# Modulation rows in four places, state space heads in another order, and inverse blocks interleaved over the array's quadrants

## What is computed

```python
# block 1
proj = rms_norm(h) @ w_in
y_ssd  = ssd_mixer(...)      # 8 heads of 64, 4 chunks of 128 tokens
y_rwkv = rwkv7_mixer(...)    # 8 heads of 64, a recurrence over tokens:
#   S = S * w_t + (S a_t) b_t^T + v_t k_t^T ;  y_t = S r_t
h = h + rms_norm(concat(y_ssd, y_rwkv) @ w_out)
f = (silu(gate) * val) @ ffn_w_down      # after a depthwise conv of rms_norm(h) @ w_up
h = h + rms_norm(f)
# block 2
mod = silu(c) @ w_mod + b_mod            # 6 * 1024 numbers for shifts, scales and gates
h = h + gate1 * hybrid_mixer(rms_norm(h) * (1 + scale1) + shift1)
h = h + gate2 * experts(rms_norm(h) * (1 + scale2) + shift2)
```

## Time and profile before

| | |
|---|---|
| runs of the kernel | 2032.84, 2038.69, 2039.38 us; median 2038.69 |
| profiled execution, its own time | 2028.1 us |
| its span | 2026.3 us |
| busy share of the span | TensorE 89%, weight loads 69%, VectorE 60%, GpSimd 34%, ScalarE 24% |
| mean granted clock of TensorE | 0.923 |

### The profile page before, as it was taken

How to read it: one execution, slowest core, us unless ns; L and a number is a source line. 1 busy time by engine, 2 the same in 40 slices (tenths; PEclk the granted TensorE clock), 3 DMA queues, 4 the chain that set the end, 5 groups by cost and what they waited for, 6 DMA issues and landing times.

```text
span 2026.3 us, 28621 instructions
## 1 busy us (share of the span) xinstructions
PE 1812.8 (89%) x11514; PEld 1393.4 (69%) x11514; DVE 1224.7 (60%) x1599; ACT 491.4 (24%) x734; POOL 679.9 (34%) x383
## 2 busy tenths in 40 slices
PE   6999666998887999999979999989898998699998
PEld 4888345777665777777738788877676775466665
DVE  6959236564438888888760276728734442566664
ACT  2121322442112111101131111312133103354443
POOL 2664000000152666666526556004433562100000
PEclk8999567999798999999989999659999999799999
DMA  5231222222023222322212222001311225488884
GB/s 196 83 104 63 83 84 66 105 86 97 14 80 115 87 101 83 103 83 89 77 42 84 83 83 83 1 1 63 120 42 63 83 84 207 178 348 343 333 334 176
DMA packets 34066, 230.47 MB, mean 114 GB/s; under 512 B 4132, under 2 KB 4388, under 8 KB 8232
## 3 DMA queue, kind: packets, MB, share of 16 engines
q1 hardware_dynamic: 30240, 214.48, 29.2%
q10 hardware_dynamic: 2136, 10.24, 1.3%
q0 software_dynamic: 1584, 4.21, 0.6%
HBM read 220.98 MB, written 9.50 MB: 114 GB/s over the span
## 4 chain that ended last, share of the span: by engine, by line
PE 73%; DVE 15%; DMA 5%; ACT 3%; issue 3%; POOL 0%; SPq 0%; DVEq 0%; ACTq 0%; POOLq 0%
PE psum L383 72%; DVE arena L1465 4%; DVE arena L1471 4%; DMA arena<-units 2%; DVE arena L1468 2%; DMA weight_ring<-units 2%; PE psum L387 1%; ACT arena L1119 1%; DVE tiny L1479 1%; ACT L1119 1%; DVE expert_lo L1465 1%; ACT expert_hi L1119 0%; ACT tiny L1119 0%; DMA arena<-x 0%; POOL slots L2321 0%
## 5 line engine op out<-in xcount | busy, mean ns | idle before, releaser
L1119 ACT ACTIVATE arena<-psum 128x512 f32<-128x512 f32 (+4 forms) x295 | 149.2, 520 | 901.0 <-PE psum L383 789.8
L383 PE MATMUL psum<-arena 64*64 64x64 f32 (+4 forms) x2828 | 270.4, 290 | 59.9 <-DVE arena L1465 45.7
L383 PEld LDWEIGHTS psum<-arena 64*64 64x64 f32 (+3 forms) x2828 | 194.9, 171 | 117.6 <-issue 67.1
L383 PE MATMUL psum<-normed_hi,w_in_hi 128*128 128x512 f32 x512 | 204.3, 399 | 14.3 <-DVE in_lo L1465 8.3
L1465 DVE TENSOR_TENSOR arena<-arena,psum 128x512 f32<-128x512 f32 (+2 forms) x200 | 112.2, 588 | 151.8 <-PE psum L383 103.5
L383 PE MATMUL psum<-normed_hi,w_in_lo 128*128 128x512 f32 x512 | 203.3, 397 | 0.0
L383 PE MATMUL psum<-in_lo,w_in_hi 128*128 128x512 f32 x512 | 201.8, 394 | 0.0
L1471 DVE SCALAR_TENSOR_TENSOR arena<-arena,fixed_data 128x512 f32<-128x512 f32 x134 | 188.9, 1410 | 13.5 <-DVE arena L1468 0.2
L2279 POOL TENSOR_TENSOR w_ff_lo<-weight_ring,w_ff_hi 128x1024 fp32r<-128x1024 f32 x66 | 166.6, 2524 | 5.5
L2279 POOL TENSOR_TENSOR w_in_lo<-weight_ring,w_in_hi 128x1024 fp32r<-128x1024 f32 x64 | 163.1, 2548 | 5.4
L383 PE MATMUL psum<-arena,fixed_data 128*128 128x512 f32 (+10 forms) x424 | 130.6, 474 | 36.4 <-DVE arena L1465 18.0
(11 more groups left out here) (226 smaller groups left out, 3527.2 us busy)
## 6 DMA issues: line engine op xcount, KB each, us to landing
weight_ring<-units SPq DMA_DIRECT2D x124, 1024.0 KB, 4.8
arena<-units SPq DMA_DIRECT2D x55, 1024.0 KB, 7.5
normed<-units SPq DMA_DIRECT2D x20, 1024.0 KB, 8.1
slots<-arena ACTq DMA_DIRECT2D x7, 516.0 KB, 5.1
arena<-slots SPq DMA_DIRECT2D x7, 516.0 KB, 5.8
fixed_data<-fixed ACTq DMA_DIRECT2D x1, 2944.0 KB, 12.0
arena<-x SPq DMA_DIRECT2D x4, 512.0 KB, 5.9
arena<-bias_rows ACTq DMA_DIRECT2D x2, 896.0 KB, 5.7
```

The source lines that it names most:

```text
L383: return nc.tensor.matmul(o, l, r, start=start, stop=stop)
L1119: return nc.scalar.activation(o, i, func, **kw)
```

## The change

- **Modulation**: of the 24 units, 10 stand in the state space stage (two ahead of the loop, then one behind each head's 7 matmuls), 10 in the pairs (levels 2 and 4; in the fourth pair levels 1 to 4), 2 behind the sum after the output projection and 2 behind the sum after the feed-forward (`last_modulation`, with its own row buffers and its own columns). SyncE's order of loads follows: the last four units are taken out of their place in memory when their turn comes. GpSimd begins to split the feed-forward's weights, and later those of the second projection, when the second of these rows is in PSUM, where it waited for the last tile of the output projection or of the feed-forward.
- **State space heads**: `cs_row(h + 2)` stands ahead of head h's matmuls, `s_HB` has four buffers, the other right-hand side is written in place, ScalarE and VectorE run `decay_row` and `log_decays` two heads ahead.
- **Pairs**: a transposed copy of the first gram is computed as one more gram (`abT_crossed`, 16 matmuls of 64 x 64), with its output halves crossed; U is computed from half to other half, Z U from a half to the same half and X U from a half to the other, and Z U and X U of one head alternate, two matmuls each. `gt` and `hh` alternate in the same way, behind a wait for `aww`. VectorE makes the same number of operations.
- The four MEMSETs stand ahead of the squares of the output projection.

```diff
+            def last_modulation(g):
+
+                for j in range(2):
+                    rows_of_unit(N_MOD1 + 2 * g + j, W_MOD2_UNITS[g] + j, 5 + j)
+                o = open_("mod_columns", g, 7)
+                for j in range(2):
+                    emptied(pe, "mod_rows", N_MOD1 + 2 * g + j)
+                    for c in range(2):
+                        last = mm(o[:, 2 * j + c:2 * j + c + 1], mod_rows2[j][:, c * P:(c + 1) * P], sel4[:, :])
+                close(last, "mod_columns", g)
 
+            modulation(0)
+            modulation(1)
             for h in range(8):
                 m, e = h // 2, h % 2
-                modulation(h)
+                if h + 2 < 8:
+                    cs_row(h + 2)
                 if e == 0:
...
-                if h + 2 < 8:
-                    cs_row(h + 2)
+                modulation(2 + h)
                 if 1 <= h < 6:
                     prepare(0, h, 4)
             for g in range(2):
...
+            def block(o, q, e, t, l, r):
+
+                return mm(c8(o)[rows_of(q[1]), t, :], c8(half(l, e))[rows_of(q[0]), t, :], c8(half(r, e))[rows_of(q[0]), t, :])
...
+                        o = open_((f"U{lv}", m), e, 3 * e)
+                        for t in range(NT):
+                            for i in range(2):
+                                last = block(o, (1 - i, i), e, t, r_LV, r_X)
+                        close(last, (f"U{lv}", m), e)
...
                         emptied(pe, (f"U{lv}", m), e)
-                        blocks(f"ZU{lv}", m, e, 3 * e + 1, r_U, r_Z)
+                        oz = open_((f"ZU{lv}", m), e, 3 * e + 1)
                         if lv < 5:
-                            blocks(f"XU{lv}", m, e, 3 * e + 2, r_Z, r_U)
+                            ox = open_((f"XU{lv}", m), e, 3 * e + 2)
+                        for t in range(NT):
+                            for i in range(2):
+                                z = block(oz, (i, i), e, t, r_U, r_Z)
+                            if lv < 5:
+                                for i in range(2):
+                                    x = block(ox, (i, 1 - i), e, t, r_Z, r_U)
+                        close(z, (f"ZU{lv}", m), e)
+                        if lv < 5:
+                            close(x, (f"XU{lv}", m), e)
                     if m < 3:
                         prepare(m + 1, lv, 6)
...
                 emptied(pe, "awa", m)
-                o = open_("gt", m, 2)
+                emptied(pe, "aww", m)
+                og, oh_ = open_("gt", m, 2), open_("hh", m, 5)
...
             def decay_row(h):
                 filled(act, "cs_row", h)
                 f(xn[:, h, :], PSB[bank_of("cs_row", h)], ACT.Exp).then_inc(sem("row_decay_ready"), 1)
 
+            decay_row(0)
+            decay_row(1)
+            mod_row(0)
+            mod_row(1)
             for h in range(8):
-                decay_row(h)
                 emptied(act, "cs_row", h)
-                f(A(s_HB + (h % 2) * T), A(s_HB + (h % 2) * T), ACT.Exp).then_inc(sem("pair_decay_ready"), 1)
+                f(A(s_HB + (h % 4) * T), A(s_HB + (h % 4) * T), ACT.Exp).then_inc(sem("pair_decay_ready"), 1)
+                if h + 2 < 8:
+                    decay_row(h + 2)
                 if 2 <= h < 7:
                     prepare(0, h - 1)
-                mod_row(h)
+                mod_row(2 + h)
             for m in range(4):
                 f(proj(ZZ + m), proj(ZZ + m), ACT.Silu).then_inc(sem("z_ready"), 1)
             for g in range(2):
@@ -1239,8 +1279,8 @@
                         evac((f"U{lv}", m), e, half(r_U, e), PSB[bank_of((f"U{lv}", m), e)][:, 0:256])
                     if lv == 1:
                         evac("wv", m, r_WV)
-                    if lv < 5:
-                        mod_row(8 + 4 * m + lv - 1)
+                    if lv in (2, 4) or (m == 3 and lv in (1, 3)):
+                        mod_row(10 + 2 * m + (lv - 1 if m == 3 else lv // 2 - 1))
                     if m < 3:
                         prepare(m + 1, lv)
...
             for h in range(8):
-                if h + 1 < 8:
-                    log_decays(h + 1)
                 dve.wait_ge(sem("pair_decay_ready"), h + 1)
-                tt(A(s_CE + (h % 2) * T), proj(CM + h // 4), xn[:, h, :], ALU.mult)
-                tt(A(s_HB + (h % 2) * T), A(s_HB + (h % 2) * T), A(s_GT + (h // 4) * T), ALU.mult)\
+                tt(xn[:, h, :], proj(CM + h // 4), xn[:, h, :], ALU.mult)
+                tt(A(s_HB + (h % 4) * T), A(s_HB + (h % 4) * T), A(s_GT + (h // 4) * T), ALU.mult)\
                     .then_inc(sem("mt_ready"), 1)
+                if h + 2 < 8:
+                    log_decays(h + 2)
                 if h >= 2:
...
-                masked_gram("abT", m, r_AT, k_strict)
+                masked_gram("abT", m, r_Z, k_level[0])
+                masked_gram("abT_crossed", m, r_AT, k_strict)
                 for e in range(2):
                     emptied(dve, ("abT", m), e)
-                link(tt(c8(r_Z), c8(r_AT), rep8(k_level[0]), ALU.mult))
+                link(tt(c8(r_Z), c8(r_Z), rep8(k_ident), ALU.add))
                 masked_gram("ab", m, r_X, k_level0t)
-                link(tt(c8(r_Z), c8(r_Z), rep8(k_ident), ALU.add))
+                for e in range(2):
+                    emptied(dve, ("abT_crossed", m), e)
                 for e in range(2):
                     emptied(dve, ("ab", m), e)
...
 
+            V.memset(A(F_UB, 4 * PADW).rearrange("p (t c) -> p t c", t=4)[:, :, 0:3], 0.0).then_inc(sem("ffn_zeroed"), 1)
+            link(V.memset(A(F_ACC, 4096), 0.0))
+            link(V.memset(A(F_CMB, ROW), 0.0))
+            V.memset(A(F_CMB + D + 4, 1).bitcast(I32), T).then_inc(sem("empty_row_ready"), 1)
             for k in range(KT):
                 emptied(dve, "mix", k)
                 tt(sq(k), n_(k), n_(k), ALU.mult).then_inc(sem("sq_post_mix"), 1)
             rstd("sum_post_mix", 1.0 / D, 1e-6)
             add_normed(n_, "g_post_mix")
-            V.memset(A(F_UB, 4 * PADW).rearrange("p (t c) -> p t c", t=4)[:, :, 0:3], 0.0).then_inc(sem("ffn_zeroed"), 1)
-            link(V.memset(A(F_ACC, 4096), 0.0))
-            link(V.memset(A(F_CMB, ROW), 0.0))
-            V.memset(A(F_CMB + D + 4, 1).bitcast(I32), T).then_inc(sem("empty_row_ready"), 1)
+            def last_mod(g):
+
+                c = slice(40 + 4 * g, 44 + 4 * g)
+                filled(dve, "mod_columns", g)
+                tt(mod[:, c], PSB[7][:, 0:4], S("b_mod", 40 + 4 * g, 4), ALU.add).then_inc(freed("mod_columns", g), 1)
+
+            last_mod(0)
             rstd("sum_pre_ffn", 1.0 / D, 1e-6)
             scaled_parts(in_ff, lambda k: S("g_pre_ffn", k), "ffn_in_ready")
...
 
-            unit[0] += N_MOD
+            unit[0] += N_MOD1
 
             filled(pool, "ry_w", 3)
             split_units(w_out1, 4)
 
-            filled(pool, "mix", KT - 1)
+            unit[0] += 2
+            filled(pool, "mod_rows", N_MOD1 + 1)
             split_units(w_ff, 3 * NF)
-            filled(pool, "ffn_down", ("last", 0, KT - 1))
+            unit[0] += 2
+            filled(pool, "mod_rows", N_MOD1 + 3)
             split_units(w_in2, 18)
 
             pool.wait_ge(sem("gla_out_ready"), 4)
```

105 lines of the change are left out of this document (59 added, 46 removed).

## The result

The changed kernel takes 2010.65 us (median of four runs, 2002.60 to 2015.99) against 2035.76 (2032.33 to 2039.38) for the kernel before, run beside it: a ratio of 0.9873, 95% interval 0.9827 to 0.9919. The forecast was 2003, the range 1984 to 2020. The gain forecast was 35.6 us; the medians show 25, and the two profiled executions 22.2 (spans 2026.3 and 2004.1). So the sign and the range hold, and about a third of the gain is missing. The runs of the changed kernel spread over 13 us, those of the kernel before over 7. Repeated later, the changed kernel took 2011.77 beside 2029.92 for the kernel before: 18.2 us less, half of the forecast.

The account below looks back on a forecast made before the run. TensorE was taken to bound the kernel, holding 73% of the chain of waits. Heads -22, pairs -21, output projection +2 and feed-forward +5.4 sum to -35.6 us: 2003 against the median of 2038.69, range 1984 to 2020.

Parts of the forecast that it names:

- the place where VectorE should start (275.1): Behind the state space heads: VectorE starts at 275.1 instead of 297.1, minus 22 us (ends minus 5.5, minus 32).
- the collision: Behind both projections: GpSimd's weight splits slow VectorE's additions, 2.8 us a chunk, plus 5.5 and 5.4; bounds nothing and 5.6.
- First head at 213: State space stage: the first head's matmuls start some 1.2 us earlier than the 214.22 of before.
- The seven ways in 55 us: State space loop, first to last head's matmuls: 55 us instead of 79.6, between 47 all high clock and 70 all low.
- the circle at the high clock: State space heads at 2.4 GHz: matmuls, modulation, ScalarE's copy and exponential, VectorE's two products follow each other in 5.9 us.
- the rival of the low clock: State space heads stay TensorE's own work at 1.2 GHz and win only 5.5 us: 2019.5; chance 0.12.
- The end, 4.1 to 5.4 us: Behind head 7: VectorE waits 4.1 to 5.4 us for modulation, copy, table switch and first silu, instead of 0.1.
- The pairs, minus 21: Head pairs: minus 6.5 us for each of the first three, minus 1.3 for the fourth; bounds 13 and 25.
- its fall as a rival: Head pairs: more gaps bring TensorE down to 1.2 GHz, 27 us a pair, 2111 with all four; chance 0.02.
- Four quadrants, 1.16 us for 64 records: Pairs' levels: Z U and X U in four quadrants run at the grams' 1.16 us instead of 2.02, minus 0.8.
- The rival with the shared banks: Pairs: four quadrants with shared banks do not run side by side, 14 us less gain: 2017; chance 0.1.
- MEMSETs, minus 3.4: Behind the output projection: MEMSETs leave VectorE's path, so the next norm starts at 617.2 instead of 620.59, minus 3.4 us.

Follow-up runs that it names:

- the later splits: Changed kernel with GpSimd's first splits for the feed-forward and second projection waiting until VectorE has added the last modulation's columns; median 2007.91 us, ratio 0.9874.

## Why the prediction was right, and where its sizes were off

- **The range and the sign** hold, and the range by luck in part. The likeliest values were too good: 35.6 us against 22.2 in the profile. Against the place where VectorE should start (275.1) 4.2 us are missing, in the pairs 3.3, in the two chains 1.8 and 1.4, and 2.7 at the end: 13.4. Two of the bounds did not hold either: each chain was to lose at most 5.6 us to the collision, and it lost 5.9. What brought the forecast to within 8 us of the median is the base it counts from. The kernel before had a median of 2038.69 then, 2035.76 beside the changed kernel, and 2029.9 to 2031.5 in the four later groups of runs. As a gain, the range goes from 18.7 to 54.7 us (with every way at the high clock the heads sum to minus 31, not minus 32): the first comparison gives 25, the repetition 18.2, just outside.
- **First head at 213.** It started at 216.5. The step "the first head starts some 1.2 us earlier than now" left out that the second modulation ahead of the loop waits 2.59 us for its unit and that ScalarE has its row ahead of the first exponential. With one modulation ahead it is 212.6.
- **The seven ways in 55 us.** The first profile gives 55.3, but six others of the same loop 60.8 to 66.6. The step that failed is the reason I gave against the low clock, "a TensorE without idle time runs at 1.00 in the pairs": in the loop it was busy for 19.93 of 20 us at 0.50. The parts were right: TensorE's own work at the low clock was put at 10.2 us and is 9.9; the circle at the high clock was put at 5.9 and is 5.7 to 7.1. "I take 55, nearer to the high end" should have been 61 or so, and the rival of the low clock holds for most of the loop in most runs. Taken alone, that is 6 to 7 us of the forecast in most executions; in the profiled one the term hit.
- **The end, 4.1 to 5.4 us.** It was 4.2 with the last modulation at the high clock and 5.3 at the low one, and 0.1 with the copy behind the silus.
- **The pairs, minus 21.** They won 17.7: 7.9, 4.9, 4.3 and 0.6 us. Up to U of level 2, -2.5 + 0.7 were reckoned. In the second pair, at the high clock, that holds: the masks come 0.8 later and level 1 wins 2.95 (7.10 to 4.15). In the third pair it won only 0.6: behind the wait of 2.15 us for the masks TensorE was granted 0.62 from 390.4 to 394.6, and level 1 took 5.66 us; in the repeated kernel 5.67. The sum had the high clock everywhere in the pairs, and its fall as a rival with 0.02; a small part of that rival came true. Levels 2 to 4 of the third pair won 4.6 where 3.9 were reckoned; the rest lost 1.0 where 0.8 were to be won. The last is the step I had no row for: a wait of 1.16 us behind a late packet of instructions, and the wait for `aww`, 1.00 instead of 0.60, against which the merged groups won 0.75.
- **Four quadrants, 1.16 us for 64 records.** Measured 1.10. The rival with the shared banks falls.
- **MEMSETs, minus 3.4.** Measured 3.4 alone. In the changed kernel 1.4 of it is taken back: from the last addition to the inversion it is 3.5 us, not 2.1, since TensorE's sum comes later and partly at the low clock.
- **The collision, plus 5.5 and 5.4.** Measured 5.9 and 5.9 with two chunks inside the additions, 2.9 a chunk, and 3.8 in ten of 18 chains, where the split starts 0.1 us later or more. The net was 3.8 instead of 2, and 6.8 instead of 5.4, for the same late sum; in the repeated kernel 0.1 and 3.5. That the additions take 1.4 us each, as I wrote for the later splits, was a misreading of merged rows: single ones take 2.8.
- **Nothing was reckoned for the experts**, and 2.7 us were lost there, within the spread of that stretch.

## What to carry to other kernels

Work moved as filler costs what it takes at the clock of the place it is moved to: a modulation takes TensorE 2.8 us in a full loop at 1.2 GHz and 1.5 us in the pairs at 2.4 GHz (though two pairs that got one more grew by 3.2 and 3.7), so the idle places come first and a full loop last. When a loop's length depends on the clock, compare single edits by their place in the trace, and forecast the median from several profiles, not from one. Behind each moved step ask which queue it stands in: here a copy behind the last modulation and ahead of a table switch cost 4.2 to 5.2 us, and a split that runs beside the additions 2.9 us a chunk.

## What the hardware showed that was not expected

- TensorE was busy for 40 us with 0.07 us of idle time and was granted 1.2 GHz all the time.
- TensorE stopped for 0.25 to 2.1 us, 29 times in 13 profiles, each time until 2.0 to 2.9 us behind a 16 KB packet of the instruction queue, 27 times right behind the landing of a 1 MB unit (DMA busy 0.96), and in no pair during which no unit was loaded. Behind all six stops of 1.7 us and more, and behind one of 1.06, the clock fell to 0.50 for 3 to 10 us; behind the others it stayed at 1.00 for the next 8 us.
- A product or addition of VectorE beside a split of GpSimd ends 0.5 to 0.6 us behind GpSimd's operation, whether that leaves it 1.5 or 2.8 us long.
- Groups of 64 x 64 matmuls that use other quadrants than the group ahead of them overlap with its end: 1.49 us for 64 records against 2.02, with no alternation by two; 1.10 with it.
